# Two row tables of a chunked mLSTM, spread over all partitions by DMA instead of by matrix products

## The reference

```python
def mlstm(q, k, v, i_pre, f_pre):
    ...
    d_log = jnp.where(causal, bt[..., :, None] - bt[..., None, :] + it[..., None, :], -jnp.inf)
    inter_log = bt + m_st[..., None]
    m_t = jnp.maximum(inter_log, jnp.max(d_log, axis=-1))
    w_intra = jnp.exp(d_log - m_t[..., None])
    ...
    den = jnp.sum(sc, axis=-1) + w_inter * jnp.einsum('bhtd,bhd->bht', qt, n_st)
    h_t = num / jnp.maximum(jnp.abs(den), jnp.exp(-m_t))[..., None]
```

## Time and profile before

| | |
|---|---|
| median of 3 runs | 917.83 us (915.16 to 919.26) |
| the profiled execution | 915.55 us |
| its span | 914.2 us |
| mean granted TensorE clock | 0.988 of full |
| PE busy | 866.1 us, 95% of the span |
| DVE busy | 414.5 us, 45% |
| ACT busy | 301.3 us, 33% |
| share of the DMA queue of SP | 77.2% of 16 engines |

### The profile page before, as it was taken

One profiled execution on the slowest core, in us unless ns is written; L12 is line 12 of the kernel. 1 busy time (PEld: TensorE's weight loads), 2 busy tenths in 40 slices (PEclk: granted clock), 3 DMA queues, 4 the chain that ended last, 5 costly groups with the idle time before them and its releaser, 6 DMA issues.

```text
span 914.2 us, 12405 instructions
## 1 busy us (share of the span) xinstructions
PE 866.1 (95%) x5152; PEld 563.9 (62%) x5152; DVE 414.5 (45%) x802; ACT 301.3 (33%) x544; POOL 10.3 (1%) x14
## 2 busy tenths in 40 slices
PE   5999999999998989988899899999999999999997
PEld 3568875434454424442344333498978999887997
DVE  3196953111211102101121011289798878888973
ACT  4253142111111101110111011265546675627572
POOL 0001000000000000000000000000100000000000
PEclk9999999999999999999999999999999999999999
DMA  9999989999999999999999999664314444332431
GB/s 377 421 429 424 360 350 427 411 429 428 427 425 429 428 425 428 428 425 431 427 428 427 427 428 422 286 262 155 127 52 186 162 162 191 148 139 92 141 139 47
DMA packets 25546, 291.40 MB, mean 319 GB/s; under 512 B 2832, under 2 KB 3344, under 8 KB 4240
## 3 DMA queue, kind: packets, MB, share of 16 engines
q1 hardware_dynamic: 25488, 290.58, 77.2%
HBM read 289.52 MB, written 1.05 MB: 318 GB/s over the span
## 4 chain that ended last, share of the span: by engine, by line
PE 69%; DMA 23%; DVE 6%; issue 1%; SPq 1%; ACT 1%; DVEq 0%
PE bank L1427 22%; DMA ring<-in_expert_w 17%; PE bank L1003 16%; PE bank L1035 8%; PE bank L1451 4%; PE bank L388 3%; DMA more<-in_expert_w 3%; DMA ring<-in_ada_w 3%; PE bank L935 2%; PE bank L975 2%; DVE X L358 2%; PE bank L431 2%; PE bank L404 1%; PE bank L1475 1%; PE bank L1603 1%; DVE halves L1328 1%
## 5 line engine op out<-in xcount | busy, mean ns | idle before, releaser
L1003 PE MATMUL bank<-ring,xg 128*64 128x512 f32 x768 | 238.1, 603 | 16.5 <-DMA ring<-in_expert_w 16.5
L1427 PE MATMUL bank<-HH,halves 128*128 128x256 f32 x848 | 164.5, 289 | 0.0
L1003 PEld LDWEIGHTS bank<-ring,xg 128*64 128x64 f32 x768 | 75.2, 139 | 136.1 <-issue 107.7
L1427 PEld LDWEIGHTS bank<-HH,halves 128*128 128x128 f32 x848 | 135.7, 192 | 5.9 <-issue 4.8
L1003 PE MATMUL bank<-more,xg 128*64 128x512 f32 x256 | 119.7, 621 | 7.8 <-DMA more<-in_expert_w 7.8
L1427 PE MATMUL bank<-HL,halves 128*128 128x256 f32 x424 | 120.4, 284 | 0.0
L1122 DVE TENSOR_TENSOR X<-X,bank 128x512 f32<-128x512 f32 x16 | 11.0, 687 | 231.0 <-PE bank L1003 231.0
L1035 PE MATMUL bank<-ring,X 128*64 128x512 f32 x384 | 113.3, 595 | 0.7 <-ACT X L1075 0.7
L1328 DVE TENSOR_TENSOR halves<-raw,halves 128x1024 fp32r<-128x1024 f32 (+1 forms) x84 | 91.9, 1129 | 6.3 <-ACT halves L1320 6.3
L1135 DVE SCALAR_TENSOR_TENSOR ygL<-bank,small,ygH 128x512 fp32r<-128x512 f32 x32 | 24.0, 751 | 132.9 <-ACT ygH L1082 132.9
L1427 PEld LDWEIGHTS bank<-HL,halves 128*128 128x128 f32 x424 | 81.7, 193 | 0.7 <-issue 0.5
(11 more groups left out here) (345 smaller groups left out, 1204.0 us busy)
## 6 DMA issues: line engine op xcount, KB each, us to landing
ring<-in_expert_w SPq DMA_DIRECT2D x68, 2048.0 KB, 26.9
more<-in_expert_w SPq DMA_DIRECT2D x22, 2048.0 KB, 26.0
raw<-in_units SPq DMA_DIRECT2D x38, 1024.0 KB, 4.8
ring<-in_ada_w SPq DMA_DIRECT2D x10, 2048.0 KB, 20.9
ring<-in_expert_w SPq DMA_DIRECT2D x8, 1024.0 KB, 30.4
ring<-in_w_in SPq DMA_DIRECT2D x3, 2048.0 KB, 34.8
more<-in_ada_w SPq DMA_DIRECT2D x2, 2048.0 KB, 27.8
ring<-in_w_out SPq DMA_DIRECT2D x2, 2048.0 KB, 21.9
```

Of the source, the lines that this page charges most:

```text
L1003: t = pe.matmul(bank[3 + i][64 * x:64 * x + 64, :], xg[q % 2][:, k, o + 64 * x:o + 64 * x + 64], place(at[x])[:, k, :], start=k == 0, stop ...
L1427: t = pe.matmul(ps[:, T * j:T * j + T], part(x[:, k, 128 * j:128 * j + 128]), part(y[:, k, :]), start=first and a == 0, stop=last and a == ...
```

## The change

In place of the six products of a layer (L1500, L1501, and four of L1509; each shows as two matmul records) SP issues eight DMAs: four copy one row of rM (1 KB of one partition) into all 128 partitions of `mrow`, four copy one row of rB into 64 partitions of `srow`. Both lie in places of `scr` that are unused at that time. The issues stand on SP's queue ahead of the load of unit 10, behind waits for `s_gate`. `stab_exp` and `m_log` read SBUF instead of PSUM and wait for all four DMAs of their table. `m_scores(0)` comes after `tile(7, 0)`. The waits of TensorE that belonged to the products are gone.

```diff
@@ -1243,6 +1243,7 @@
             av, bcv = (v3(scr[:, 6672 + 1024 * i:7696 + 1024 * i], 2) for i in range(2))
             br, bt, tmp4 = (v3(scr[:, 8720 + 1024 * i:9744 + 1024 * i], 4) for i in range(3))
             squares = v3(scr[:, 3600:5648], 8)
+            mrow, srow = v3(scr[:, 5648:6672], 4), v3(scr[:, 6672:7184], 2)
 
             root, first, mean, rcol = (small[:, a:a + 2] for a in (314, 316, 318, 312))
             spread = v3(rt[:, :], 2)
@@ -1389,8 +1390,20 @@
                 for k in range(8):
                     low_of(0, k)
 
+            def rows_sp(l):
+
+                sp.wait_ge(s_gate, 23 * l + 22)
+                for h in range(4):
+                    sp.dma_start(mrow[:, h, :], rM[h:h + 1, :].unsqueeze(1).broadcast_to([1, 128, T])).then_inc(s_mM, 16)
+                sp.wait_ge(s_gate, 23 * l + 23)
+                for h in range(4):
+                    o = 64 * (h % 2)
+                    sp.dma_start(srow[o:o + 64, h // 2, :], rB[h:h + 1, :].unsqueeze(1).broadcast_to([1, 64, T])).then_inc(s_stab, 16)
+
             def second_sp():
                 for U in range(6, 2 * NU):
+                    if U % NU == U_AV:
+                        rows_sp(U // NU)
                     sp.wait_ge(s_unit, NU if ahead(U) else U - 3)
                     sp.dma_start(unit_place(U), unit_source(U)).then_inc(unit_signal(U), 16)
                 for i in range(4):
@@ -1496,18 +1509,6 @@
                     pe.wait_ge(s_gate, 23 * l + 23)
                     pe.matmul(bank[2][:, 0:4], rg[:, 0:128], ident[0:4, 0:4], start=True, stop=True)
                     pe.matmul(bank[2][:, 4:8], rg[:, 128:256], ident[0:4, 0:4], start=True, stop=True).then_inc(s_gcT, 1)
-                    pe.wait_ge(s_rs, 12 if l else 9)
-                    pe.matmul(bank[6][:, 0:T], con("selp", 0, 128)[0:4, :], rB, start=True, stop=True)
-                    pe.matmul(bank[6][:, T:2 * T], con("selp", 128, 128)[0:4, :], rB, start=True, stop=True).then_inc(s_stab, 1)
-
-                def m_rows(l, j):
-                    if j:
-                        pe.wait_ge(s_mW, 8 * l + 4)
-                    else:
-                        pe.wait_ge(s_gc, l + 1)
-                    for x in range(2):
-                        pe.matmul(bank[2][:, T * x:T * x + T], con("selm", 256 * j + 128 * x, 128)[0:4, :], rM,
-                                  start=True, stop=True).then_inc(s_mM, 1)
 
                 def m_scores(l, j):
                     if j:
@@ -1669,10 +1670,8 @@
                     tile(l, 6, 0)
                     stabilisers(l)
                     tile(l, 6, 1)
-                    m_rows(l, 0)
+                    tile(l, 7, 0)
                     m_scores(l, 0)
-                    tile(l, 7, 0)
-                    m_rows(l, 1)
                     tile(l, 7, 1)
                     m_out(l, 0)
                     m_scores(l, 1)
@@ -1768,8 +1767,8 @@
                         act.activation(dst[:, i, :], unit_bank(l, u + i)[:, :], ACT.Copy, scale=rcol[:, i:i + 1]).then_inc(signal, 1)
 
                 def stab_exp(l):
-                    act.wait_ge(s_stab, l + 1)
-                    act.activation(flat(em), bank[6][:, :], ACT.Exp, scale=-1.0).then_inc(s_em, 1)
+                    act.wait_ge(s_stab, 64 * l + 64)
+                    act.activation(flat(em), flat(srow), ACT.Exp, scale=-1.0).then_inc(s_em, 1)
 
                 def m_exp(l, h):
                     for i, (a, z) in enumerate(((0, 256), (256, 384))):
@@ -2001,9 +2000,9 @@
                     yield
 
                 def m_log(l, h):
-                    ps = bank[2][:, T * (h % 2):T * (h % 2) + T]
+                    ps = mrow[:, h, :]
                     dve.wait_ge(s_late, 16)
-                    dve.wait_ge(s_mM, 4 * l + 2 * (h // 2) + 2)
+                    dve.wait_ge(s_mM, 64 * l + 64)
                     if h >= 2:
                         dve.wait_ge(s_mX, 4 * l + h - 1)
                     dve.scalar_tensor_tensor(X1[:, h % 2, 0:256], ps, -1.0, con("mneg"), ALU.mult, ALU.add).then_inc(s_mW, 1)

```

## The result

| | before | after |
|---|---|---|
| median | 917.36 us, 4 runs (915.16 to 919.26) | 959.73 us, 4 runs (958.64 to 962.38) |
| profiled execution | 915.55 us, span 914.2 | 959.36 us, span 958.0 |
| mean granted clock | 0.988 | 0.965 |

The ratio of the times is 1.0472, 95% interval 1.0452 to 1.0492: slower by 42 us. The forecast was 967.4.

A forecast was written before the change was run, and what follows sets the result against it. TensorE, busy 95% of the span, was taken to bound the kernel. Products won, stalls and lower clock, −6.3 + 52.7 + 3.2 = +49.6 us on the median of 917.83, gave 967.4 us, range 915 to 990.

The forecast's parts named there:

- The removed products: On TensorE's queue in the last two layers: products taken away win 3.14 us for a layer, 6.3 us for two.
- The move costs nothing: `m_scores(l, 0)` behind `tile(l, 7, 0)`: scores end at 640.6 in layer 0, VectorE weighs them only at 641.99, so no cost.
- One place's rate: Rows read out of one SBUF partition run at one engine's share, 26.8 GB/s, taking 29.4 us a layer; chance 0.68.
- The stall: TensorE waits at `m_out(0)` for the late rows: 26.4 us in layer 0, 26.3 in layer 1, together 52.7.
- The clock: After each stall TensorE's granted clock is lower for a while, costing 1.6 us for each, 3.2 together.
- SP's queue: Eight issues on SP's queue take at most 3.5 us from 631.8, so unit 10's issue, near 636.7, is not late.
- The sum: Whole kernel: products won, stalls and lower clock, −6.3 + 52.7 + 3.2 = +49.6 us.
- The middle rival: Rows at several engine shares or a fixed cost for each DMA: 921 us at 1 us each, 938 at two shares; chance 0.15.
- The full-rate rival: One partition reads as fast as any; rows land at 639.8 and 793.8, no stall, 911.5 us; chance 0.17.

The follow-up runs named there:

- The kernel with the late `stab_exp`: Kernel before with only the stabiliser's rows by DMA, its two products gone, and `stab_exp` moved behind all four `m_exp`: 915.33 us, ratio 0.9981.
- the split one: Against the kernel before: products for the maximum of heads 0 and 1, DMAs for its heads 2 and 3 and the stabiliser, readers later: 913.2 us, ratio 0.9964.
- the wide source: Changed kernel with the same eight DMAs per layer reading ones, each partition its own row, maximum and stabiliser left out: 915.81 us, ratio 0.999 to before.
- the runs with chosen partitions: Four variants of the changed kernel reading rows of ones out of partitions 0 and 1, 0 and 64, or 0, 32, 64, 96: 937.3 to 959.94 us.
- four places in each DMA: Changed kernel, all DMAs on SP, each reading ones out of partitions 0, 32, 64 and 96, a quarter of the rows from each: 937.3 us.
- One row of HBM: Changed kernel with each DMA reading one 1 KB row of ones in HBM 128 (64) times, maximum and stabiliser left out: 929.35 us, ratio 1.0133 to before.
- 0 and 64 on two queues: Changed kernel with half the DMAs on SP reading ones out of partition 0, half on POOL out of partition 64: 948.07 us.
- one place for each head: Changed kernel, all DMAs on SP, each reading ones out of one partition, 32 h for head h: 947.46 us.
- both kernels with two queues: Changed kernel with half the DMAs on SP out of partition 0, half on POOL out of partition 1 or 64, reading ones: 959.94 and 948.07 us.

## Why the prediction was right, and where its numbers were off

- **The removed products, −6.3.** Right as a price of TensorE's time. The kernel with the late `stab_exp` won 1.7 us (0.7 to 2.8 by the interval) for 2.06 us of them, the split one 3.3 (2.1 to 4.4) for 4.2 less 1.1 of wait. In the kernel after they are more than used up by the wait.
- **The move costs nothing.** Shown by the kernel with the move alone.
- **One place's rate, 26.8 GB/s, from the source.** The rate was 26 to 28, and the wide source shows that the source is the cause. The reason that I gave, "what carries a stream through one place is one engine's share", was right in size only, and that is luck: one sixteenth of the whole rate is what a group of partitions gets too. The step before it was misread. The loads that reach 428 read HBM and write to 128 partitions, so the earlier trace rows said nothing about how many partitions a fast source needs. I had added that the figure would hold if one engine did it all; the engines' share of 0.8 in all windows says that this isn't what happens, and the runs with chosen partitions put the limit on a group of partitions.
- **The stall, 26.4 + 26.3 = 52.7.** This is the term that was mis-sized: 46.1, or 23.0 and 23.2 for a layer. In layer 0 the rows were there at 663.56 and not at 667.4; from there to `m_out` it took 2.72 us, where 2.63 were forecast. (Layer 1 runs later as a whole by the first stall.) Of the 3.8 us, 2.5 are the transfer: the 768 rows took 26.9 us and not 29.4, since the first 85 went much faster than the 27 to 28 GB/s of the rest. 0.6 are the start, at 636.4 and not at 637.0; SP issued the loads of units 8 and 9 from 629.88 in this execution and not from 630.3, and the rows began when these were nearly through, as forecast. 0.7 are the landing, 0.3 us behind the last row and not 1.0.
- **The clock, 1.6 for each stall.** 1.8 measured in layer 0 and 2.0 in layer 1, by the 4.1 and 4.3 us of the group of products that took 2.3 before.
- **SP's queue, 3.5 us for eight issues, unit 10 not late.** Wrong. The issues of the stabiliser's rows were held up to 13.75 us and took 21.96 together, so unit 10's load was issued at 655.95 and not near 636.7. It did no further harm: no wait of ScalarE for a load follows in that stretch, since TensorE stood still as well. In the kernel with the split, where TensorE runs on, a little of it is seen: one issue of a unit's load takes 4.96 us from 636.63 and ScalarE waits 3.10 us for a unit before 656.92, where it waited 1.96 before 651.62 in the kernel before. TensorE does not wait for it.
- **The sum.** −6.3 + 46.1 + 3.8 = +43.6. The spans differ by 43.8.
- **The middle rival's sum.** At 1 us for each DMA I had −6.3 + 9.9 = +3.6, with no term for the clock, though the wide source lost 1.7 us of full clock behind a wait of 2.3. With 3.2 for both layers it would have been +6.8, or 924.6.
- **The full-rate rival, 911.5.** Its condition did not come, and the wide source, which comes nearest to it, gave 915.81. Its rows took 4.7 us (637.6 to 642.3) where I had put 1.8, and were 2.2 us late, where I had put their landing at 639.8. With its source in all partitions and everything else as it is, this change was worth nothing measurable.

## What to carry to other kernels

A broadcast by DMA out of one partition (or several neighbours) ran at some 27 GB/s here, with 64 or 128 partitions as its target and with all 16 DMA engines free for it; put its bytes through that rate before taking it for free, and compare with the products that it replaces (here 27 us against 3). Where such a row must be spread, use only what fits before its reader, read it from partitions of two groups (0 and 64 here), and put the instruction that waits for it behind everything on its engine that the critical path needs. If an issue can be held up, every load behind it on the same queue is late as well.

## What the runs showed that I had not expected

- An SP issue can stand for 13.75 us: from the fifth of eight such DMAs on, the issues took 21.96 us instead of some 2.5. With the wide source the same four took 2.77, and with four places in each DMA 9.13:

```profile
634.32 2.77 SPq L1401 DMA_DIRECT2D scr<-cst  x4
```

- One row of HBM read again and again gives 70 to 85 GB/s, more than one place of SBUF.
- A wait of only 2.3 us for a layer was followed by the clock's lower level, 1.7 and 1.6 us of full clock: hardly less than behind a wait of 23 us (1.8 and 2.0).
- A second queue puts the rows beside the loads, and the loads pay for it. With 0 and 64 on two queues POOL's rows begin at 638.0, and the loads of units 8 and 9, issued from 632.29, are through at 641.9. With one place for each head, where the rows stand behind them in one queue, they are issued from 632.06 and through at 639.0. A window of the kernel with two queues in which they still move:

```profile
639.00:640.00 1.00, 1.00 (x10) 0.96 (x8) 1.00 (x1) 0.98 (x2) 0.00 (x0) 1.00 0.68 98
```

- In both kernels with two queues, where `stab_exp` waits for two semaphores in a row, its table load came after the wait and lay on the path:

```profile
662.68 1.28 ACT L1774 ACT_TABLE_LOAD   x1 [23.39 <-DMA scr<-cst]
```
